# The state-space scan and the gated short convolution's three weight tiles in one block, the result split in the up-projection's block

## The reference

```python
def short_conv_mixer(gate_b, gate_c, h, conv_w):
    return gate_b * causal_dwconv(gate_c * h, conv_w)        # 256 wide, 3 taps

def ssd_scan(xdt, a_dt, bh, ch):                             # chunks of 128, 4 heads
    a_cs = jnp.cumsum(a_dt..., axis=-1)
    decay_in = jnp.exp(jnp.where(tri, diff, -jnp.inf))
    scores = jnp.einsum("bclhn,bcshn->bhcls", ch, bh) * decay_in
    y_diag = jnp.einsum("bhcls,bcshp->bclhp", scores, xdt)
    chunk_states = jnp.einsum("bclhn,bclhp->bchpn", bh * decay_to_end[..., None], xdt)
    ...                                                      # scan over chunks: state * dec + st
    y_off = jnp.einsum("bclhn,bchpn->bclhp", ch, prev) * decay_from_start[..., None]
```

## Time and profile before

| | us |
|---|---|
| median of 3 runs | 2669.24 |
| lowest, highest | 2666.09, 2671.38 |
| profiled execution | 2669.09 |
| its span, first to last instruction | 2667.4 |

### The profile page before, as it was taken

One profiled execution on the slowest core, in us unless ns is written; L12 is line 12 of the kernel. 1 busy time (PEld: TensorE's weight loads), 2 busy tenths in 40 slices (PEclk: granted clock), 3 DMA queues, 4 the chain that ended last, 5 costly groups with the idle time before them and its releaser, 6 DMA issues. The chain is left out here.

```text
span 2667.4 us, 32886 instructions
## 1 busy us (share of the span) xinstructions
PE 2446.6 (92%) x13072; PEld 1993.8 (75%) x13072; DVE 1243.6 (47%) x1735; ACT 986.2 (37%) x2095; POOL 628.2 (24%) x289
## 2 busy tenths in 40 slices
PE   3798999898998999887999968998999999999998
PEld 2586787676877777776878866677778888888886
DVE  4793401684562521484544156561644333333436
ACT  3223422474522432375422355553622222222223
POOL 2211111132321122032232120111323323232331
PEclk9899999898999999898999988999999999999999
DMA  7342110003212210002211000003212111111214
GB/s 207 132 134 75 54 48 32 19 14 111 79 41 71 72 48 32 16 17 95 79 64 48 11 21 5 17 13 119 80 32 63 48 48 49 46 57 39 63 33 150
DMA packets 140110, 158.74 MB, mean 60 GB/s; under 512 B 7340, under 2 KB 109107, under 8 KB 139957
## 3 DMA queue, kind: packets, MB, share of 16 engines
q1 hardware_dynamic: 137549, 152.12, 17.6%
q10 hardware_dynamic: 2408, 4.52, 0.5%
HBM read 135.65 MB, written 20.97 MB: 59 GB/s over the span
## 5 line engine op out<-in xcount | busy, mean ns | idle before, releaser
L698 PE MATMUL ps<-hT_hi,w_hi 128*128 128x512 f32 x1184 | 463.6, 392 | 23.3 <-PEq L369 12.7
L698 PE MATMUL ps<-hT_lo,w_hi 128*128 128x512 f32 x1184 | 462.6, 391 | 0.0
L698 PE MATMUL ps<-hT_hi,w_lo 128*128 128x512 f32 x1184 | 462.4, 391 | 0.0
L698 PEld LDWEIGHTS ps<-hT_hi,w_hi 128*128 128x128 f32 x1184 | 223.5, 189 | 71.1 <-issue 24.7
L698 PEld LDWEIGHTS ps<-hT_hi,w_lo 128*128 128x128 f32 x1184 | 223.4, 189 | 46.6
L698 PEld LDWEIGHTS ps<-hT_lo,w_hi 128*128 128x128 f32 x1184 | 223.4, 189 | 46.4
L634 POOL TENSOR_TENSOR w_lo<-ffn_raw,w_hi 128x2048 fp32r<-128x2048 f32 (+1 forms) x32 | 163.7, 5114 | 112.9 <-ACT w_hi L608 112.9
L3590 DVE TENSOR_SCALAR work<-work,fcols 128x1024 f32<-128x1024 f32 x44 | 33.2, 755 | 287.4 <-ACT work L3547 287.4
L3547 ACT ACTIVATE work<-ps 128x512 f32<-128x512 f32 x88 | 52.3, 596 | 280.5 <-PE ps L698 273.8
L608 ACT ACTIVATE w_hi<-ffn_raw 128x2048 fp32r<-128x2048 f32 (+1 forms) x32 | 59.7, 1864 | 246.4 <-PE ps L698 145.3
L3571 POOL TENSOR_TENSOR ffn_hid_lo<-work,ffn_hid_hi 128x1024 fp32r<-128x1024 f32 x22 | 64.9, 2949 | 345.9 <-ACT ffn_hid_hi L3561 345.9
(11 more groups left out here) (493 smaller groups left out, 5227.4 us busy)
## 6 DMA issues: line engine op xcount, KB each, us to landing
ffn_raw<-in_ffn_w_up SPq DMA_DIRECT2D x40, 512.0 KB, 5.2
mix_gla<-in_w_ada SPq DMA_DIRECT2D x32, 512.0 KB, 3.7
big<-xres SPq DMA_DIRECT2D x3, 4096.0 KB, 16.2
xres<-big SPq DMA_DIRECT2D x24, 512.0 KB, 2.6
difp_raw<-in_w_in SPq DMA_DIRECT2D x10, 1024.0 KB, 5.0
ffn_raw<-in_ffn_w_down SPq DMA_DIRECT2D x10, 1024.0 KB, 5.0
ada_raw<-in_w_ada SPq DMA_DIRECT2D x16, 512.0 KB, 5.3
gla_wraw<-in_w_in SPq DMA_DIRECT2D x8, 1024.0 KB, 5.9
```

The costliest lines, as they stand in the source:

```text
L698: mm = nc.tensor.matmul(out, l, r, start=(job.part != 1 and c == 0 and k == 0), stop=(job.evac and c == job.chunks - 1 and k == 2))
```

## The change

The three tiles of the short convolution go to the end of the mixer's list of jobs. scc is still loaded and split by the projection (`hold`), but all 288 matmuls of the three tiles now run in the scan's block, as 24 half units of 12 matmuls: first half of the contraction for four banks, then the second half, tile by tile (`unit`). Four come in front, and two in each of the steps 0 to 9. For that the scan keeps to four PSUM banks (TURN, SCORE, DECAY, STATE) and the fillers take the other four. The scan's pieces are spread over steps n to n + 3: TensorE transposes chunk n, makes scores, the earlier part of chunk n - 1, turns the result of chunk n - 3, then makes state and inner part of chunk n - 1. ScalarE empties scc's units (`empty_c`), VectorE those of sch with the taps (`empty_h`) and of scb (`empty_b`); `t1` gets two buffers and the skip product moves to the inputs. Tiles sch and scb are loaded and split within the block (`ScanWeights`), the up weights later than before (steps 6 to 8). The scan's output is left unsplit in `feat`'s rows 0 and 1; its split, and that of `yconv`, are done in the up-projection's block by ScalarE (four copies, ahead of units 8, 10, 12 and 14) and POOL (four subtractions). In that block the rotary tables and token tiles change places in `m.big`; the tables wait for POOL's first two, and VectorE's first r product for all four.

```diff
-    F_JOBS = (("scc", C_SCC), ("sch", C_SCH), ("scb", C_SCB), ("xbc", C_XBC), ("xbc", C_XBC + WCOLS),
-              ("xbc", C_XBC + 2 * WCOLS))
-    jobs = [Job(tag, wtile(w, c0, WCOLS), KC, WCOLS, "F", spread=(n == 0)) for n, (tag, c0) in enumerate(F_JOBS)]
-    return jobs + halved("zcq", [wtile(w, C_Z, SSD_DIM), wtile(w, 0, QLORA)], SSD_DIM + QLORA) + [
-                   Job("ckvdt", [wtile(w, C_KV, KVLORA + ROPE), wtile(w, C_DT, SSD_H)], KC, KVLORA + ROPE + SSD_H,
-                       "T")]
-def stage_mixer_project(nc, m, jobs, yconv, feat, lat, z, dt, base, block, opening):
-    G_CONV = 12
+    def tile(tag, c0, **kind):
+        return Job(tag, wtile(w, c0, WCOLS), KC, WCOLS, "F", **kind)
+    jobs = [tile("xbc", C_XBC + WCOLS * n, spread=(n == 0)) for n in range(3)]
+    jobs += halved("zcq", [wtile(w, C_Z, SSD_DIM), wtile(w, 0, QLORA)], SSD_DIM + QLORA)
+    jobs.append(Job("ckvdt", [wtile(w, C_KV, KVLORA + ROPE), wtile(w, C_DT, SSD_H)], KC, KVLORA + ROPE + SSD_H, "T"))
+    return jobs + [tile("scc", C_SCC, hold=True), tile("sch", C_SCH), tile("scb", C_SCB)]
...
-        def split(dve, i):
-            fi = f[:, i % 2, :].rearrange("p (c t) -> p c t", c=2)
-            hi, lo = m.hT_hi[:, 6:8, P * i:P * i + P], m.hT_lo[:, 6:8, P * i:P * i + P]
-            dve.wait_ge(s_f, i + 1)
-            nc.vector.tensor_copy(hi, fi).then_inc(s_hi, 1)
-            dve.wait_ge(s_hi, i + 1)
-            nc.vector.tensor_tensor(lo, fi, hi.bitcast(F32), ALU.subtract).then_inc(s_lo, 2)
         @block.gpsimd
         def _(pool):
-            for c in range(2):
-                pool.wait_ge(s_chi, c + 1)
-                pool.tensor_tensor(m.hT_lo[:, 4 + c, :], yconv[:, c, :], m.hT_hi[:, 4 + c, :].bitcast(F32),
-                                   ALU.subtract).then_inc(s_clo, 1)
-            weights.low(pool)
+            tiles.low(pool)
+            ups.low(pool)
         @block.sync
         def _(sp):
-            weights.load(sp)
+            load_tile(sp, tiles.raw, tiles.jobs[0], tiles.s_raw)
+            ups.load(sp)
+            sp.wait_ge(tiles.s_lo, 1)
+            load_tile(sp, tiles.raw, tiles.jobs[1], tiles.s_raw)
...
+            def project(u):
+                job, k, second = unit(u)
+                if u in (8, 16):
+                    pe.wait_ge(tiles.s_lo, u // 8)
+                if job == 1 and not second:
+                    pe.wait_ge(s_cev, k + 1)
+                if job == 2 and not second:
+                    pe.wait_ge(s_us, k + 1)
+                sub, half = k // 2, k % 2
+                cols, toks = slice(P * sub, P * sub + P), slice(512 * half, 512 * half + 512)
+                hi, lo = (w[:, slots[job], :].rearrange("p (c n) -> p c n", c=KC) for w in (m.w_hi, m.w_lo))
+                for c in range(KC // 2 * second, KC // 2 * second + KC // 2):
+                    a_hi, a_lo = m.hT_hi[:, c, toks], m.hT_lo[:, c, toks]
+                    for t, (l, r) in enumerate(((hi[:, c, cols], a_hi), (hi[:, c, cols], a_lo), (lo[:, c, cols], a_hi))):
+                        mm = nc.tensor.matmul(ps[:, FILL + k, :], l, r, start=(c == 0 and t == 0),
+                                              stop=(c == KC - 1 and t == 2))
+                if second:
+                    mm.then_inc(s_unit, 1)
+                elif u == 19:
+                    mm.then_inc(s_kslot, 1)
...
+            for u in range(LEAD):
+                project(u)
+                if u == 1:
+                    pe.wait_ge(s_adt, 1)
+                    for k, tri in enumerate((m.tri_up, m.tri_low, m.ones)):
+                        mm = nc.tensor.matmul(cum[k], tri[:, :], adt[:, :, :], start=True, stop=True)
+                    mm.then_inc(s_cum, 1)
+            for n in STEPS:
+                units = steps_units(n)
+                if n < NT:
+                    turn(n)
+                if units:
+                    project(units[0])
+                if n < NT:
+                    scores(n)
+                if 1 <= n - 1 < NT:
+                    earlier(n - 1)
+                if n >= 3:
+                    turn_y(n - 3)
+                if units:
+                    project(units[1])
+                if 0 <= n - 1 < NT - 1:
+                    states(n - 1)
+                if 0 <= n - 1 < NT:
+                    inside(n - 1)
...
+            for n in STEPS:
+                if n < NT:
+                    decays(n)
+                if 0 <= n - 2 < NT:
+                    norm(n - 2)
+                if n >= 3:
+                    empty_y(n - 3)
+                if n == 0:
+                    tiles.high(act, 0)
+                for u in steps_units(n):
+                    if u < 8:
+                        empty_c(unit(u)[1])
+                if n < NT:
+                    keys = lat.ckv[:, n, 0:KVLORA]
+                    nc.scalar.activation(keys, keys, ACT.Copy, scale=lat.r[:, 1, n:n + 1])
+                if n == 2:
+                    tiles.high(act, 1)
+                if n == 6:
+                    act.wait_ge(s_unit, 2 * SUBS)
+                if n == 8:
+                    act.wait_ge(s_kslot, 1)
+                for k in {6: range(0, 4), 7: range(4, 8), 8: range(8, 10)}.get(n, ()):
+                    ups.high(act, k)
...
+            def empty_h(k):
+                sub, cols = k // 2, slice(512 * (k % 2), 512 * (k % 2) + 512)
+                pad = SC_K - 1
+                dve.wait_ge(s_unit, SUBS + k + 1)
+                dve.wait_ge(s_cev, k + 1)
+                if k == 2:
+                    dve.wait_ge(s_conv, SC_K)
+                nc.vector.tensor_tensor(us[:, pad + cols.start:pad + cols.stop], ps[:, FILL + k, :], yconv[:, sub, cols],
+                                        ALU.mult).then_inc(s_us, 1)
+                if k % 2:
+                    dve.wait_ge(s_pad, 1)
+                    dve.wait_ge(s_us, k + 1)
+                    for j in range(SC_K):
+                        tap = m.bcols[:, m.B_SCW + 2 * j + sub:m.B_SCW + 2 * j + sub + 1]
+                        if j == 0:
+                            nc.vector.tensor_scalar(yconv[:, sub, :], us[:, 0:S], tap, None, ALU.mult).then_inc(s_conv, 1)
+                        else:
+                            dve.wait_ge(s_conv, SC_K * sub + j)
+                            nc.vector.scalar_tensor_tensor(out=yconv[:, sub, :], in0=us[:, j:j + S], scalar=tap,
+                                                           in1=yconv[:, sub, :], op0=ALU.mult,
+                                                           op1=ALU.add).then_inc(s_conv, 1)
+            def empty_b(k):
+                sub, cols = k // 2, slice(512 * (k % 2), 512 * (k % 2) + 512)
+                dve.wait_ge(s_unit, 2 * SUBS + k + 1)
+                dve.wait_ge(s_conv, SC_K * (sub + 1))
+                nc.vector.tensor_tensor(yconv[:, sub, cols], ps[:, FILL + k, :], yconv[:, sub, cols],
+                                        ALU.mult).then_inc(s_bev, 1)
+            for n in STEPS:
+                if n < NT:
+                    inputs(n)
+                    decayed(n)
+                if 1 <= n - 1 < NT:
+                    earlier(n - 1)
+                if 0 <= n - 1 < NT - 1:
+                    states(n - 1)
+                if 0 <= n - 1 < NT:
+                    output(n - 1)
+                if 0 <= n - 2 < NT:
+                    normed(n - 2)
+                for u in steps_units(n):
+                    job, k, second = unit(u)
+                    if second and job == 1:
+                        empty_h(k)
+                    if second and job == 2:
+                        empty_b(k)
...
+    MIXED_AT = (8, 10, 12, 14)
...
+        for n, (c, row) in enumerate(mixed):
+            pool.wait_ge(s_mhi, n + 1)
+            pool.tensor_tensor(m.hT_lo[:, c, :], big[:, row, :], m.hT_hi[:, c, :].bitcast(F32),
+                               ALU.subtract).then_inc(s_mlo, 1)
...
+            if u in MIXED_AT:
+                n = MIXED_AT.index(u)
+                nc.scalar.activation(m.hT_hi[:, mixed[n][0], :], big[:, mixed[n][1], :], ACT.Copy).then_inc(s_mhi, 1)
...
+                stage_mixer_project(nc, m, mixer[:-2], feat, lat, z, dt, 1, block, opening)
...
+                          mixer[-3:], (1, 0, 1))
```

More of the change, by code:

```diff
@@ L933, in low @@
     def low(self, pool):
-        for k in range(4):
+        for k in range(len(self.jobs)):
             pool.wait_ge(self.s_hi, k + 1)
@@ L2333, in stage_mixer_project @@
-    by = {"scc": "A", "sch": "V", "scb": "V", "xbc": "AV"}
-    stage_project(nc, m, "mixp", jobs, m.hT_hi, m.hT_lo, act_unit, dve_unit, lambda job: by.get(job.tag, "A"),
-                  extra="pad tap conv silu sc lat", setup=setup, dve_before=dve_before, base=base, block=block,
-                  opening=opening)
+        if u[1] == 1:
+            conv.dve(dve, q, halves_of(job, g, u), 2 * jobs.index(job) + u[0])
+    stage_project(nc, m, "mixp", jobs, m.hT_hi, m.hT_lo, act_unit, dve_unit,
```

(31 more changed lines are left out.)

295 lines of the change are left out of this document (124 added, 171 removed).

## The result

The changed kernel took 2642.45 us (median of four runs, 2638.73 to 2642.86) against 2668.93 for the kernel before (four runs, 2666.09 to 2671.38): a ratio of 0.9898, 95% interval 0.9881 to 0.9915. Five more runs gave 2642.41 (2637.07 to 2645.23), ratio 0.9904 (0.9889 to 0.9919). The profiled execution took 2642.26, 26.8 less than the profiled one of before (26.9 by the two spans); the forecast's sum said 18.7 less.

The account below looks back on a forecast made before the run. TensorE, busy 92% of the span, bounds the kernel, except in the scan's block, paced by a chain over three engines. -65.3 + 43.6 + 1 + 2 = -18.7 from 2669.1 gives 2650; forecast 2645 to 2656, wide range 2642 to 2660.

Parts of the forecast that it names:

- the scan's own matmuls: In the scan's block: eight chunks at 4.6 us, less 0.9 for the first, 35.9 us; bounds 4.4 and 4.84 a chunk.
- term 2: Scan's block: TensorE's queue becomes the bound, and the block grows from 65.6 to 109.2 us, +43.6.
- term 3: Scan's block: POOL's two added tile splits hold VectorE and stall TensorE, +1 us; bounds 0 and 10.
- term 4: Up-projection's block: ScalarE's four added split copies stall TensorE by 1.9 us, partly given back; +2 us, bounds -1 and +5.
- Term 1: Projection: 288 matmuls of three weight tiles leave, -65.3 us; the split of scc that stays costs nothing.
- Lead and sums: Start of the scan's block: 48 matmuls in four units, slow at first, 13.4 us, and cumulative sums 0.9 us.
- Units: Scan's block: 20 units of 12 matmuls between scan pieces, 2.90 us each, 58.0 us in all.
- Tail: Scan's block: entry 0.1 us, and one ScalarE copy with its latency behind the last transposes 0.9 us, together 1.0.
- The warm start: Start of the up-projection's block: 24 transposes no longer slowed after the scan's idle times, giving back 0.5 to 1 us.
- the clean overlap: Rival: cheaper scan pieces and units, warm lead, no stall, unchanged up block; -27.8 us, 2641; chance 0.12 for 2641 to 2645.
- VectorE held by POOL: Rival: stalls at two tile splits and two convolution steps in the scan's block, 10 us; 2659, up to 2663; chance 0.22.
- The uncovered chain: Rival: TensorE reaches each scan piece before VectorE has finished, filler covers nothing; 2677; chance 0.04 slower, 0.03 within 0.2%.

## Why the prediction was off

The direction, the mechanism and the bound were right: the filler lies beside the chain, TensorE's queue becomes the limit, and no step waits. The step that failed is the size of the scan's own matmuls in term 2 (4.6 us a chunk, measured 4.00), together with the stall of term 3 (1, measured 0) and the one of term 4 (+2, measured -1.7); all three were priced too high, and one stretch that I held constant moved the other way.

- **Term 1, projection: right.** -65.3 forecast, -64.9 measured, the last matmul at 1471.3 where I said 1472. The tile scc costs nothing there.
- **Term 2, the scan's own matmuls: mis-sized, the largest miss.** "A drained pipeline at each of the three waits is in it (...), so I take 4.6". I named the effect and then took off 0.24 of 4.84 for it. A wait costs 0.23 us beside its idle time (4.23 against 4.00 above; 0.23 to 0.27 by the pieces of the step of before), so three are 0.7 to 0.8, and the measured 4.00 lies below my lower bound of 4.4. By the block's parts: 102.84 - 14.06 (lead and sums) - 56.8 (20 x 2.84) - 1.35 (tail) = 30.6, where I had 35.9: 5.3 us. The rule for it stands in the Trainium skill ("TensorE: Matmul & The Clock Gate", section "Step-by-step: what each phase is for"): the end of one matmul overlaps with the start of the next, and a single one can't hide it. The trace agrees; idle time isn't the whole price of a wait.
- **Term 2, the rest.** Lead and sums 14.06 against 14.3: right, and eleven matmuls came 0.43 us apart as forecast. Units 2.84 against 2.90: 1.2 us over 20. The row that I took the earlier trace rows is the first scan's, with other small matmuls around it. Tail 1.35 against 1.0.
- **Term 3, stalls: there was none.** The count of slack held at both places. At n = 2 POOL stretched VectorE's addition to 4.84 us and TensorE didn't see it. In the convolution steps I counted half a microsecond of slack; TensorE came to `states` at 1544.34 and `earlier` ran from 1543.63 to 1544.04, 0.3 us ahead. A delay of 2.79 us there cost 2.72. So the +1 was a price for a risk, taken from a stall of 2.5 by no rule, and wrong as a sum; that no wait came at so thin a margin was in part luck.
- **Term 4, up-projection: a wrong reading.** "ScalarE has nothing to give there: it empties eight units in 5.39 us and eight in 5.50, TensorE's own pace." A row whose instructions run at the producer's pace shows the producer. ScalarE's own time for a unit is 0.48, so it gives 0.2 us a unit, and the four copies fit. The stall of 1.9 and its slow stretch of 1.6 didn't come. (The sum was loose too: 1.9 + 1.6, less 0.5 to 1, is 2.5 to 3, and I took 2.) The Trainium skill ("ScalarE: Activation LUTs", section "What ACT_TABLE_LOAD costs") would have told me: 186 ns and 0.833 ns an element, less 93 back to back, which makes 0.52 for 512 elements (an estimate by that page); the trace has 0.48 to 0.51. The warm start was there and larger than my 0.5 to 1: the 24 transposes took 2.94 us, start to start, at a clock of 1.00, against 4.63 at 0.54 before, and that is the block's whole -1.7.

```profile
1579.23 2.81 PE L2915 MATMUL ps<-ident,v 128*128 128x128 f32 x24 [0.97 <-PEq L2365]
1582.17 0.47 PE L2896 MATMUL ps<-kr_hi,w_hi 128*128 128x512 f32 x1
```

- **Attention: not in the sum.** +3.1 in this pair of traces, by the clock's lower stretches. It is the only large miss in the other direction, and it hid part of the others: without it this pair of traces would differ by 30.0. So it is luck that the time came as near to the forecast as it did.

The misses: +0.4 (projection), -0.6 (upstream), -7.4 (scan with term 3), -3.7 (up block), +3.1 (attention), together -8.2, or -18.7 to -26.9.

Of the rivals, the clean overlap (2641) was the nearest. It was right that nothing stalls, nearly right on the units, still too high on the scan's matmuls (4.4 for 4.00), and wrong on the lead, which stayed slow, and on the attention; that its sum, -27.8, comes within 1 us of the measured one is such misses cancelling. VectorE held by POOL is a true mechanism with a true price, at a place where it had cover; its waiting taps didn't occur. The uncovered chain didn't happen; even with half the filler TensorE's waits were 5.6 us in all.

## What to carry to other kernels

When a piece of work moves from an engine that waited to one whose queue is full, price it at its start-to-start times between other work, and take off the drained pipeline at each wait that goes: 0.23 us each here, which for the three waits of the step that I priced, eight times over, is 5.5 us, more than both stalls in my sum. Before an engine is called full, look whether its pace is its own or its producer's. And compare stages between their own boundaries: whole runs here differ by 8 us, the stages by 0.1, except where the clock falls.

## What the runs showed of the hardware

- Filler can shorten a block: with 1 matmul a unit the scan's block took 90.8 us, with 6 it took 85.5, though 100 matmuls (22.7 us at full clock) more are in it. With 1 the block had 24.8 us of waits and a mean clock of 0.80 behind the lead (0.95 with 6), so its short matmuls ran slow as well.
- A VectorE sum with one input in PSUM ran at its usual 0.42 us while POOL was subtracting; the product of two SBUF tiles right behind it took 3.22.
- The same code, from the attention on, took 1017.2 to 1020.6 us in one kernel or another, with a mean clock of its first 50 us from 0.73 to 0.86. The idle time ahead of it doesn't explain that: with 1.78 us of it the attention took 1017.7 in one kernel, with 1.77 us 1020.6 in another.
